# Picking a group's rows with rounded halves, 256 columns at a time, in a trunk with a grouped mixture of experts

## The reference

```python
def grouped_moe(x2, router_w, router_b, w_gate, w_up, w_down):
    scores = jax.nn.sigmoid((x2 @ router_w).astype(jnp.float32))
    sel = (scores + router_b).reshape(n_tok, N_GROUPS, EXPERTS_PER_GROUP)   # 8 groups of 4 experts
    group_score = lax.top_k(sel, TOP_K)[0].sum(-1)
    _, g_idx = lax.top_k(group_score, 1)                                    # one group for a token
    ...                                                                     # its two best experts, and their gates
    def expert_block(args):
        h = jax.nn.silu(xblk @ w_gate[e]) * (xblk @ w_up[e])                # 1024 -> 512
        return h @ w_down[e]                                                # 512 -> 1024
    ...
    return jnp.zeros_like(x2).at[tok_buf].add(yb * gate_buf[:, None])
...
        x = layer_norm(ALPHA * x + m, ln2_g[i], ln2_b[i])
```

## Time and profile before

| | |
|---|---|
| time, median of 3 executions | 1594.22 us (1593.18 to 1595.34) |
| the profiled execution | 1596.03 us, with a span of 1594.20 from first to last instruction |
| PE busy | 1426.5 us (89%) |
| DVE, ACT, POOL busy | 501.1, 282.2, 52.8 us |
| DMA | 463.72 MB, mean 291 GB/s |
| mean granted clock of TensorE | 0.945 |
| L985, gate and up products | 466.1 us in 2048 instructions |
| L1025, down products | 234.3 us in 1024 |
| L967, the turns | 136.2 us in 512 |
| expert phases | first gate_up at 258.63 and 1103.43 us; second half of gate_up(31) at 723.47 and 1566.03 |

### The profile page before, as it was taken

One profiled execution on the slowest core, in us unless ns is written; L12 is line 12 of the kernel. 1 busy time (PEld: TensorE's weight loads), 2 busy tenths in 40 slices (PEclk: granted clock), 3 DMA queues, 4 the chain that ended last, 5 costly groups with the idle time before them and its releaser, 6 DMA issues. The chain is left out here.

```text
span 1594.2 us, 16020 instructions
## 1 busy us (share of the span) xinstructions
PE 1426.5 (89%) x6550; PEld 791.4 (50%) x6550; DVE 501.1 (31%) x1028; ACT 282.2 (18%) x483; POOL 52.8 (3%) x66
## 2 busy tenths in 40 slices
PE   6999866999999899998799996684999999998996
PEld 5878663444343343334587875573444343333342
DVE  2355662122121221221544228654121221221221
ACT  3231420010110110111443213330010110110111
POOL 0000100000000000000000000010000000000000
PEclk9999977999999999999899988796999999999998
DMA  8530556899999999996132020436899999999992
GB/s 241 185 80 0 203 221 248 351 421 421 420 421 422 420 421 421 422 418 254 54 106 76 30 106 1 198 145 269 351 421 421 421 422 420 421 422 420 422 417 103
DMA packets 96532, 463.72 MB, mean 291 GB/s; under 512 B 10952, under 2 KB 31432, under 8 KB 47304
## 3 DMA queue, kind: packets, MB, share of 16 engines
q1 hardware_dynamic: 91848, 454.26, 70.6%
q0 software_dynamic: 4608, 8.40, 1.4%
HBM read 458.44 MB, written 12.58 MB: 295 GB/s over the span
## 5 line engine op out<-in xcount | busy, mean ns | idle before, releaser
L985 PE MATMUL bank<-ring,xT 128*64 128x512 f32 x2048 | 466.1, 608 | 37.0 <-DMA ring<-in_w_up 34.9
L985 PEld LDWEIGHTS bank<-ring,xT 128*64 128x64 f32 x2048 | 144.8, 139 | 311.9 <-issue 266.6
L1025 PE MATMUL bank<-ring,hidT 128*64 128x512 f32 x1024 | 234.3, 599 | 1.1 <-issue 1.1
L1204 DVE COPY xT<-bank 128x512 f32<-128x512 f32 x64 | 44.3, 692 | 539.7 <-PE bank L967 539.7
L967 PEld LDWEIGHTS bank<-x_sb 128*128 128x128 f32 x512 | 124.2, 327 | 71.2 <-issue 48.7
L967 PE MATMUL bank<-x_sb 128*128 128x128 f32 x512 | 136.2, 413 | 22.3 <-DMA x_sb<-x_rows,tok_of_slot 22.3
L1025 PEld LDWEIGHTS bank<-ring,hidT 128*64 128x64 f32 x1024 | 67.8, 136 | 157.1 <-issue 156.9
L1128 ACT ACTIVATE hid<-bank 128x256 f32<-128x256 f32 x64 | 24.5, 383 | 497.1 <-PE bank L985 497.1
L1134 ACT COPY y<-bank 128x512 f32<-128x512 f32 x64 | 37.5, 586 | 384.1 <-PE bank L1025 384.1
L1214 DVE COPY hidT<-bank 128x256 f32<-128x256 f32 x64 | 27.1, 423 | 180.1 <-PE bank L999 180.1
L1042 PE MATMUL bank<-y,x_sb 64*128 64x512 f32 x256 | 72.3, 641 | 2.2 <-ACT y L1134 1.4
(11 more groups left out here) (270 smaller groups left out, 1442.5 us busy)
## 6 DMA issues: line engine op xcount, KB each, us to landing
ring<-in_w_down SPq DMA_DIRECT2D x62, 2048.0 KB, 20.9
ring<-in_w_gate SPq DMA_DIRECT2D x60, 2048.0 KB, 22.1
ring<-in_w_up SPq DMA_DIRECT2D x60, 2048.0 KB, 30.1
ring<-in_mlstm_w_in SPq DMA_DIRECT2D x6, 2048.0 KB, 7.7
ring<-in_conv_w_in SPq DMA_DIRECT2D x18, 512.0 KB, 6.2
ring<-in_w_out SPq DMA_DIRECT2D x2, 4096.0 KB, 14.3
ring<-in_w_gate SPq DMA_DIRECT2D x8, 1024.0 KB, 15.5
ring<-in_w_up SPq DMA_DIRECT2D x8, 1024.0 KB, 26.6
```

The source lines that it names most:

```text
L985: last = nc.tensor.matmul(GU_BANK[e % 2][64 * f:64 * f + 64, :], xgT[e // 2 % 2][:, 4 * h + c, 64 * (e % 2):64 * (e % 2) + 64], gu[:, :, h ...
L1025: last = nc.tensor.matmul(Y_BANK[e % 2][64 * n:64 * n + 64, :], hidT[e % 2][:, c, 64 * f:64 * f + 64], dn[:, f, c, 512 * n:512 * n + 512], ...
L1204: V.tensor_copy(xgT[q % 2][:, 4 * h:4 * h + 4, :], o[:, :].rearrange("p (c r) -> p c r", c=4)).then_inc(xcopied, 1)
```

## The change

The first group is turned as before, but into wider tiles: its four turns (two for each pair of experts) go to three banks, and the fourth of them, turn 3, moves from behind gate_up(1) to behind gate_up(0). For the other seven groups ACT copies the gathered tile, rounded to float32r, into `rows_hi`; VectorE subtracts that from the tile into `rows_lo`, also float32r; `pick` is written as float32r. Four turns for a group now cover all four experts at once: each has two column blocks of inputs, and for each of these a product of `rows_hi` and one of `rows_lo` with all 256 columns of the group's `pick`, added up in the bank. The two halves lie over `onehot`, so the first of them waits until the gate codes have been made. Turns are placed by `fills(e)`: with n the first expert of the next group, turn n+j-1 behind gate_up(e) for j = 1, 2, 3, and turn n+3 behind down(e-1) at j = 3; none in the last group. gate_up of a group's experts waits for all four of its turns. The layer norm's vectors get tiles of their own, as `xgT` grows to twice its size, and the scratch for dynamic DMA descriptors is set to 8192 bytes per partition.

```diff
             mem_l["onehot"] = sb(f"onehot_{l}", [P, TT, N_GROUPS, SLOTS], BF16, at=at)
+            mem_l["rows_half"] = halves_at(f"rows_half_{l}", [P, D_MODEL], onehot_at, onehot_at + 4 * D_MODEL)
...
-                xgT = [flat[:, 1024 * i:1024 * (i + 1)].rearrange("p (k r) -> p k r", k=KT) for i in range(2)]
-                ln_g, ln_b = flat[:, 2048:3072], flat[:, 3072:4096]
+                xgT = [flat[:, 2048 * i:2048 * (i + 1)].rearrange("p (k r) -> p k r", k=KT) for i in range(2)]
+                ln_g, ln_b = (sb(f"ln2_{n}_{l}", [P, D_MODEL], at=ph)[:, :] for n in ("g", "b"))
...
+                X_BANKS = X_BANK, ACC[0], X_BANK, ACC[1]
+                def fills(e):
+                    j, n = e % PER_GROUP, PER_GROUP * (e // PER_GROUP + 1)
+                    if n == N_EXPERTS:
+                        return (), ()
+                    return ((2, 3) if e == 0 else (n + j - 1,) if j else ()), ((n + 3,) if j == 3 else ())
+                split_after = lambda e: e // PER_GROUP + 1 if e % PER_GROUP == 0 and e // PER_GROUP + 1 < N_GROUPS else 0
...
                         def turn_rows(k):
-                            q, h = k // 2, k % 2
-                            g = q // 2
-                            if k % 4 == 0:
-                                pe.wait_ge(gathered[g % 3], 16 * (g // 3 + 1))
-                                pe.wait_ge(picked, g + 1)
-                            if k >= 2:
+                            g, i = k // 4, k % 4
+                            if g == 0:
...
+                            else:
+                                if i == 0:
+                                    pe.wait_ge(rows_lo_ready, g)
+                                    pe.wait_ge(picked, g + 1)
                                 pe.wait_ge(xcopied, k)
-                            o = ACC[0] if k == 1 else X_BANK
-                            for c in range(4):
-                                last = nc.tensor.matmul(o[:, c * P:(c + 1) * P], xg[g % 3][:, 512 * h + c:512 * h + 512:4],
-                                                        pick[g % 2][:, 2 * (q % 2):2 * (q % 2) + 2, :].rearrange("p j r -> p (j r)"),
-                                                        start=True, stop=True)
+                                four = pick_r[g % 2][:, :, :].rearrange("p j r -> p (j r)")
+                                for n in range(2):
+                                    h, c = divmod(2 * i + n, 4)
+                                    cols = slice(512 * h + c, 512 * h + 512, 4)
+                                    nc.tensor.matmul(X_BANK[:, 256 * n:256 * n + 256], rows_hi[:, cols], four,
+                                                     start=True, stop=False)
+                                    last = nc.tensor.matmul(X_BANK[:, 256 * n:256 * n + 256], rows_lo[:, cols], four,
+                                                            start=False, stop=True)
                             last.then_inc(xturned, 1)
...
-                                pe.wait_ge(xcopied, 2 * (e // 2) + 2)
+                                pe.wait_ge(xcopied, 2 * (e // 2) + 2 if e < PER_GROUP else e // PER_GROUP * PER_GROUP + PER_GROUP)
...
                             gate_up(e)
-                            turn_rows(e + 2)
+                            for k in fills(e)[0]:
+                                turn_rows(k)
...
                                 down(e - 1)
+                            for k in fills(e)[1]:
+                                turn_rows(k)
...
+                        def split_rows(g):
+                            act.wait_ge(gathered[g % 3], 16 * (g // 3 + 1))
+                            if g == 1:
+                                act.wait_ge(gates_coded, 1)
+                            else:
+                                act.wait_ge(xturned, 4 * g)
+                            nc.scalar.copy(rows_hi[:, :], xg[g % 3]).then_inc(rows_hi_ready, 1)
...
+                        def split_rows(g):
+                            dve.wait_ge(rows_hi_ready, g)
+                            V.tensor_tensor(rows_lo[:, :], xg[g % 3], rows_hi[:, :], ALU.subtract).then_inc(rows_lo_ready, 1)
...
-    nc = _bacc.Bacc("TRN2", target_bir_lowering=False, num_devices=1)
+    nc = _bacc.Bacc("TRN2", target_bir_lowering=False, num_devices=1, dynamic_dma_scratch_size=8192)
```

More of the change, by code:

```diff
@@ L857, in expert_phase @@
                 xg = [x_sb[:, i, :] for i in range(3)]
-                xgT = [flat[:, 1024 * i:1024 * (i + 1)].rearrange("p (k r) -> p k r", k=KT) for i in range(2)]
-                ln_g, ln_b = flat[:, 2048:3072], flat[:, 3072:4096]
+                xgT = [flat[:, 2048 * i:2048 * (i + 1)].rearrange("p (k r) -> p k r", k=KT) for i in range(2)]
+                ln_g, ln_b = (sb(f"ln2_{n}_{l}", [P, D_MODEL], at=ph)[:, :] for n in ("g", "b"))
+                rows_hi, rows_lo = mem_l["rows_half"]
+                pick_r = [nc.alloc_sbuf_tensor_at(f"pick_r{i}_{l}", [P, PER_GROUP, BLK], F32R,
+                                                  offset=xT_at - 4 * (512 - 256 * i)) for i in range(2)]
                 gateT = [x_sb[:, 3, 256 * i:256 * (i + 1)].rearrange("p (j r) -> p j r", j=2) for i in range(2)]
@@ new lines, in turn_rows @@
+                            if g == 0:
+                                if i == 0:
+                                    pe.wait_ge(gathered[0], 16)
+                                    pe.wait_ge(picked, 1)
+                                if i == 2:
+                                    pe.wait_ge(xcopied, 2)
+                                two = pick[0][:, 2 * (i // 2):2 * (i // 2) + 2, :].rearrange("p j r -> p (j r)")
+                                for c in range(4):
+                                    cols = slice(512 * (i % 2) + c, 512 * (i % 2) + 512, 4)
+                                    last = nc.tensor.matmul(X_BANKS[i][:, c * P:(c + 1) * P], xg[0][:, cols], two,
+                                                            start=True, stop=True)
+                            else:
+                                if i == 0:
+                                    pe.wait_ge(rows_lo_ready, g)
+                                    pe.wait_ge(picked, g + 1)
+                                pe.wait_ge(xcopied, k)
+                                four = pick_r[g % 2][:, :, :].rearrange("p j r -> p (j r)")
[6 more added lines that the diff above has]
+                                                            start=False, stop=True)
@@ L1198, in rows_in @@
                         def rows_in(k):
-                            q, h = k // 2, k % 2
+                            g, i = k // 4, k % 4
                             dve.wait_ge(xturned, k + 1)
[L1201 to L1204, removed]
+                            if g >= 2:
+                                dve.wait_ge(gu_done, PER_GROUP * (g - 1))
+                            if g == 0:
+                                V.tensor_copy(xgT[0][:, 4 * (i % 2):4 * (i % 2) + 4, P * (i // 2):P * (i // 2) + P],
+                                              X_BANKS[i][:, :].rearrange("p (c r) -> p c r", c=4)).then_inc(xcopied, 1)
+                            else:
+                                V.tensor_copy(xgT[g % 2][:, 2 * i:2 * i + 2, :],
+                                              X_BANK[:, :].rearrange("p (c r) -> p c r", c=2)).then_inc(xcopied, 1)
                         def hidden(e):
@@ L1241, in _ @@
                             g, j = e // PER_GROUP, e % PER_GROUP
-                            if e + 2 < N_EXPERTS:
-                                rows_in(e + 2)
+                            for k in fills(e)[0]:
+                                rows_in(k)
                             hidden(e)
```

15 lines of the change are left out of this document (11 added, 4 removed).

## The result

The changed kernel takes 1601.99 us (median of 5 executions, 1601.12 to 1603.26) against 1595.34 us for the kernel before in the same five rounds: a ratio of 1.0046, interval 1.0034 to 1.0058. A second set, among the experiments, gave 1.0045 (1.0032 to 1.0058), without one execution of it that took 1656.81 us. So the change costs some 7 us, where +3.8 was forecast; the time lies above the range.

The account below looks back on a forecast made before the run. DMA transfers were taken to bound the expert phases, so only delays at their start and tail count: 2.06 us for the starts plus 1.7 for one slow tail, +3.8, giving 1598.0 us, range 1592.8 to 1600.5.

Parts of the forecast that it names:

- The bound: Expert phases: DMA at 421 GB/s sets the pace; after expert 3's down-matrix issue, the phase end follows down(0) one for one.
- The price of a new turn: TensorE: four rounded products of 256 columns take 1.03 us, four times the present 0.258 us spacing; the old turn takes 2.06.
- the rival built on the speed of the columns: TensorE turns: a new turn takes 0.45 us, starts cost +0.9, with one slow tail 1596.8; chance 0.08.
- The shift of down(0): Start of each phase: down(0) and the issue of expert 3's down matrix come 1.03 us later, +2.06 in two phases.
- The tail: End of each phase: 2.1 to 2.7 us of wait before gate_up(31) slows the clock in one tail, +1.7 us.
- the clock holds in both tails: Rival at the phase ends: no slow clock, only the starts count, +2.06 us, 1596.3; chance 0.20.
- Steady phase: Middle of each expert phase: PE saves 1.03 us per expert but already waits for DMA; worth 0.
- copies and subtractions: ACT and DVE, seven groups: a rounding copy of 0.99 us and a subtraction of 1.15 us, both covered; worth 0.
- gathers: Gathered rows are wanted earlier, group 3's at expert 8 instead of 10, with 12 us of margin; worth 0.
- scratch: Smaller DMA descriptor scratch: even if the second gather waits for the first, it lands before ACT asks; worth 0.
- PE's waits on w_up: Sign expected in the profile after: these TensorE waits grow from 34.9 us to 90 or more.

Follow-up runs that it names:

- a1: Changed kernel with turn 3 back behind gate_up(1) and the first rounded turn (4) behind down(0): 1595.72 us, ratio 0.9998 to the kernel before.
- a5: Changed kernel with each rounded product of the turns of groups 2 to 7 made twice: 1600.34 us, ratio 1.0029 to the kernel before.
- a7: Changed kernel with turn 2 ahead of gate_up(0), so turn 3 alone stands between the two gate_ups: 1593.96 us, ratio 0.9990 to the kernel before.
- b1: Kernel before with its float32 turn 3 moved from behind gate_up(1) to behind gate_up(0), run twice: ratios 1.0001 and 1.0004.
- b3: Kernel before with only the DMA descriptor scratch set to 8192: ratio 1.0006.
- b5: Kernel before with turn 2 ahead of gate_up(0) and turn 3 behind it: 1590.66 us, ratio 0.9973.
- a6: Changed kernel with turn 3 back behind gate_up(1), turn 4 behind down(0), and expert 4's gate and up matrices issued first: 1588.85 us, ratio 0.9968 to the kernel before.

## Why the prediction was wrong

Point by point, by its own steps:

- *The bound.* Right. From the issue of expert 3's down matrix to the last w_up it is 438.8 to 439.8 us in every kernel that keeps SP's order and lets the gap open (before, after, a1, a5, a7, b1, b3, b5).
- *The price of a new turn*, taken at 1.03 us from the spacing of strided weight loads: 1.13 to 1.15 from its first start to what follows. The load of the rounded half takes 320 and 332 ns (medians, L993 and L995), near the 330 of the earlier trace rows; the starts within a turn lie 0.34, 0.23 and 0.24 us apart. The fast loads of the Trainium skill's "TensorE: Matmul & The Clock Gate" (Weight-path perf modes) don't show for these strided float32r weights, and the rival built on the speed of the columns falls. Nor was 0.45 us what the Trainium skill's page would make of it: at the twice the speed that the prediction cites, a load of 330 ns would still take 165, an estimate of 0.66 us a turn.
- *The shift of down(0).* Right in its term of turn work, +1.03 a phase: the issue less the two gate_ups stands at 9.3 us before (25.54 - 9.15 - 7.09) and at 10.24 to 10.44 in the four phases of the two profiles after.
- *The step that failed* is that same item, where it moves gate_up(1) "2.06 later, and so does all behind it": it lets gate_up(1) keep its 7.09 us. In the four phases after it took 8.43 to 8.78, 1.3 to 1.7 more, 3.0 us together (mean 8.61 less 7.09, twice). The trace of before showed slow gate_ups behind waits alone, and I asked what waits do to the clock. That two turns, the small gate codes and 0.33 us of wait can do the same, with PE busy but for that wait, I did not ask.
- *The tail.* The wait of 2.1 to 2.7 us came (1.56 + 0.83, 1.53 + 0.85), the slow clock didn't: +1.7 forecast, 0 measured, in the two profiles and in the tails of all the experiments. The rival "the clock holds in both tails", with 0.20, came true, and with it its remark that part of the wait falls ahead of 31's first half; that the clock held because of this is not shown. This error has the other sign than the one above, so its 1.7 us brought the forecast nearer to the result by luck: without it, it would have been 1596.3.
- *Steady phase, copies and subtractions (1047 and 1224 ns), gathers and scratch at nothing.* Right, by a1, a5, a6 and b3 within their intervals. PE's waits on w_up grew to 71.9 us, not to 90: the rest went into slow gate_ups, over 20 of them in place of 7.

The sum with what was measured: T rises by 3.1 and 2.8 us in the first profile, 2.2 and 2.9 in the second, so 5.5 in the mean, of which 2.1 are turn work, 3.0 the clock of gate_up(1) and the rest lies in the transfers behind the issue (439.4 us in the mean against 439.2, twice). The times rose by 7.3 and 7.2 by the ratios. The 1.7 us between lie within the intervals; the first profile has 1.8 us more in layer 1's gate_up(0) (8.92 against 7.09), the second has 7.09. Over the 14 profiles with two turns ahead of it that gate_up was slow in 5, in 1 of the 6 of the kernel before and its edits and in 4 of the 8 of the changed kernel and its edits: too few to lay it to the change or to rule that out. That, and how little of b1's slow gate_up(1) its time shows, stays open.

## What to carry to other kernels

Where transfers set the pace, a cheaper instruction in the steady state is worth nothing and one more microsecond ahead of the first releases is worth one: look for the first place where the DMA share falls, and for what stands in the queue ahead of the load that could fill it. Here an exchange of two loads gave 0.45%, and the rewrite of the turns nothing. And turns that are gathered in one place can lower the clock of the dense products behind them: cost those at both levels.

## What the runs showed of the hardware

TensorE's clock fell although PE was never idle for more than 0.33 us between the two gate_ups: behind two float32 turns (4.0 us) and 0.95 us of gate codes a gate_up took 8.4 to 8.8 us in 12 phases of 12, behind one turn 7.09 in 15 of 16. The dense gate_up(0) ahead of it didn't prevent that, and neither did, in the profile shown, a granted clock of 1.00 in the window from 1110 to 1115, right up to it. Three turns in one piece, 5.8 us without the 0.88 us gap that follows two, were followed by a fast gate_up(0) in 4 phases of 4; with two turns and the gap it was slow in 13 of 14 in layer 0 and in 5 of 14 in layer 1. Whether the gap or the number of turns does it was not separated.
